# A row ring of fifteen slots instead of ten, and a weight ring of two blocks instead of three, in a streaming encoder layer with product-key experts

## What is computed

```
xn = rmsnorm(x);  z = xn @ w_in                       # 1024 -> 5632 columns
branch A: band attention, 8 heads of 64, own chunk of 64 and 8 chunks before, learned bias
branch B: HGRN2 gated recurrence, 4 heads, 128 x 128 state, exact chunkwise form
x = x + (sigmoid(ga) * (o_a @ w_a) + sigmoid(gb) * (o_b @ w_b)) @ w_out
PEER: q = rmsnorm(x) @ w_query; per head (8) two sets of 128 keys, top 16 of each,
      top 16 of the 256 sums -> 16 experts of 16384 per token and head, gates = softmax
      hid = gelu(x . u_tab[idx]);  out = sum over heads and experts of gate * hid * v_tab[idx]
y = rmsnorm(x + PEER)
```

## Time and profile before

| what | value |
|---|---|
| runs of the kernel (3) | 4533.14, 4541.51, 4547.78 us; median 4541.51 |
| profiled execution | 4581.09 us, span 4579.2 us |
| mean granted TensorE clock | 0.787 of full |
| busy, share of the span | TensorE 70%, VectorE 68%, GpSimd 58%, ScalarE 18% |
| DMA moved | 1408.39 MB, mean 308 GB/s |
| costliest groups | v rows on TensorE 1551.9 us; u rows on VectorE 1397.7 us; row fetches issued on GpSimd 1338.1 (v) and 1300.6 us (u); products on TensorE, L573, 775.8 us |

### The profile page before, as it was taken

How to read it: one execution, slowest core, us unless ns; L and a number is a source line. 1 busy time by engine, 2 the same in 40 slices (tenths; PEclk the granted TensorE clock), 3 DMA queues, 4 the chain that set the end, 5 groups by cost and what they waited for, 6 DMA issues and landing times. The chain is left out here.

```text
span 4579.2 us, 36423 instructions
## 1 busy us (share of the span) xinstructions
PE 3201.9 (70%) x11064; PEld 1997.1 (44%) x11064; DVE 3105.0 (68%) x6491; ACT 837.2 (18%) x2078; POOL 2656.9 (58%) x2349
## 2 busy tenths in 40 slices
PE   4968558896787567976874578858765677675555
PEld 3847314463464235643651256636432345343211
DVE  0142995647749976578579856685699765858865
ACT  1221112212111123121111222211111122111100
POOL 0001565646746676667456756575577765856776
PEclk7769657598888678987986698979876788787677
DMA  5415657989999899999998999989999999999998
GB/s 126 134 49 180 171 152 187 242 256 339 339 325 371 307 348 343 380 333 322 345 352 318 335 328 375 347 315 348 333 368 348 367 384 369 359 384 359 355 379 329
DMA packets 531664, 1408.39 MB, mean 308 GB/s; under 512 B 47952, under 2 KB 223568, under 8 KB 530704
## 3 DMA queue, kind: packets, MB, share of 16 engines
q0 software_dynamic: 317856, 1149.91, 70.2%
q1 hardware_dynamic: 211088, 246.98, 16.7%
q10 hardware_dynamic: 2528, 9.18, 0.5%
HBM read 1385.98 MB, written 19.92 MB: 307 GB/s over the span
## 5 line engine op out<-in xcount | busy, mean ns | idle before, releaser
L857 PE MATMUL PS<-ring,diag 128*128 128x512 f32 (+1 forms) x2304 | 1551.9, 814 | 963.8 <-DMA ring<-in_peer_v,idx 736.1
L557 POOL DMA_INDIRECT ring<-in_peer_v,idx x1152 | 1338.1, 1162 | 762.1 <-PE PS L857 394.1
L557 POOL DMA_INDIRECT ring<-in_peer_u,idx x1152 | 1300.6, 1129 | 721.9 <-DVE hid L1557 343.0
L1557 DVE CUSTOM_DVE_ANT_0 ring<-ring,xt 128x1024 f32<-128x1024 f32 (+1 forms) x1152 | 1397.7, 1221 | 416.3 <-DMA ring<-in_peer_u,idx 271.4
L857 PEld LDWEIGHTS PS<-ring,diag 128*128 128x128 f32 (+1 forms) x2304 | 503.0, 238 | 1733.5 <-issue 1548.6
L573 PE MATMUL PS<-xnT,wring 128*128 128x256 f32 (+2 forms) x3840 | 775.8, 364 | 131.4 <-DMA wring<-in_w_in 60.2
L1567 DVE SCALAR_TENSOR_TENSOR acc<-ring,wk,acc 128x1024 f32<-128x1024 f32 (+1 forms) x576 | 739.4, 1284 | 119.5 <-DMA ring<-in_peer_v,idx 86.1
L573 PEld LDWEIGHTS PS<-xnT,wring 128*128 128x128 f32 x3840 | 692.7, 202 | 251.3 <-issue 154.2
L543 POOL DMA_DIRECT2D xt<-xn_scr x9 | 5.5, 607 | 419.1 <-DMA xn_scr<-arena 419.0
L1173 ACT ACTIVATE diag<-ident,wk 128x128 f32<-128x128 f32 (+1 forms) x576 | 189.2, 384 | 73.4 <-issue 28.7
L577 PE MATMUL PS<-wring,xnT 128*128 128x256 f32 (+1 forms) x864 | 194.6, 384 | 8.0 <-DMA wring<-in_w_in 7.9
(11 more groups left out here) (179 smaller groups left out, 2620.3 us busy)
## 6 DMA issues: line engine op xcount, KB each, us to landing
wring<-in_w_in SPq DMA_DIRECT2D x110, 1024.0 KB
wring<-in_peer_query SPq DMA_DIRECT2D x40, 1024.0 KB
wring<-in_w_out SPq DMA_DIRECT2D x20, 1024.0 KB
ring<-in_peer_u,idx POOLq DMA_INDIRECT x1152
ring<-in_peer_v,idx POOLq DMA_INDIRECT x1152
bias<-rel_scr SPq DMA_DIRECT2D x80, 144.0 KB
wring<-in_w_branch_a SPq DMA_DIRECT2D x10, 1024.0 KB
wring<-in_w_branch_b SPq DMA_DIRECT2D x10, 1024.0 KB
```

Of the source, the lines that this page charges most:

```text
L557: pool.indirect_dma_start(ring[0:tile_rows[tn], n % R, :], None, u_tab if kind == "u" else v_tab, bass.IndirectOffsetOnAxis(ap=idx[0:tile_ ...
L857: mm = pe.matmul(PS[0:rows, 6 + half, :], diag[0:rows, seq % ND, 0:rows], ring[0:rows, n % R, 512 * half:512 * (half + 1)], start=(h == 0 ...
L1557: dve.tensor_tensor_reduce(row, row, xt[0:rows, s, :], 1.0, 0.0, ALU.mult, ALU.add, hid[0:rows, m % 2, k:k + 1]).then_inc(dve_used, 1)
```

## The change

- `R` 10 to 15 and `NW` 3 to 2. One weight block (8 KB a partition) and what the next two points free make room for five slots (20 KB a partition).
- `ND` 8 to 4: ScalarE makes diagonal j at k = max(0, 2j - 2) instead of max(0, 2j - 6).
- `idx` and `gates` keep four tiles' lists in place of nine (`LISTS`); the sample's keys and values lie in place 1 of `kT` and `v`.
- A slice holds one product instead of two, on all engines, with the cost table in the same proportion; VectorE's gating in D and G follows one product behind, not two. Stage F's first slice (the subtractions of all levels) becomes three, and the masking and the reduction of a head come into separate slices.

```diff
@@ -43,9 +43,10 @@
 CACHE = 2
-NW = 3
-R = 10
-ND = 8
+NW = 2
+R = 15
+ND = 4
+LISTS = 4
 ON_PE = frozenset(range(1, TOPK, 2))
@@ -65,13 +66,13 @@
     a = [6.0, 2.5, 0.5, 1.5, 0.5, 3.0] + [2.0] * nt
-    b = [3.5] * (4 + nt) + [2.0]
+    b = [1.7] * (8 + 2 * nt) + [2.0]
     c = [1.8] * (2 * (HA * nt + 3))
-    d = [1.5] + [2.5] * 8 + [0.5]
-    e = [3.5] * (4 + 2 * nt) + [0.5]
-    f = ([8.0, 4.5, 2.0] + [2.3, 1.5, 3.2] * HB + [1.0, 0.5, 2.0, 1.5]) * nt
-    gg = [2.5] * 8 + [0.5]
-    h = [3.5] * (2 * nt) + [0.5, 2.5, 0.5, 1.5, 3.0] + [1.5] * nt
+    d = [1.5] + [1.3] * 16 + [0.5]
+    e = [1.7] * (8 + 4 * nt) + [0.5]
+    f = ([2.5, 2.5, 3.0, 4.5, 2.0] + [2.3, 1.5, 1.2, 2.0] * HB + [1.0, 0.5, 2.0, 1.5]) * nt
+    gg = [1.3] * 16 + [0.5]
+    h = [1.7] * (4 * nt) + [0.5, 2.5, 0.5, 1.5, 3.0] + [1.5] * nt
     before = a + b + c + d + e + f + gg + h + [4.0]
@@ -257,8 +258,8 @@
         v = sb("v", [P, KV, DA])
-        kS = sb("kS", [P, CB, DEC])
-        vS = sb("vS", [P, DA])
+        kS = kT[:, :, P:P + DEC]
+        vS = v[:, 1, :]
         T12 = sb("T12", [P, 2, 2, DA])
@@ -270,8 +271,8 @@
 
-        idx = sb("idx", [P, NT * P], U32)
-        gates = sb("gates", [P, NT * P])
+        idx = sb("idx", [P, LISTS * P], U32)
+        gates = sb("gates", [P, LISTS * P])
         arena = sb("arena", [P, 5120 + 7680])
@@ -553,7 +554,7 @@
                     pool.wait_ge(dve_used if who == "dve" else pe_used, seq + 1)
-                at = tn * P + h * TOPK + k
+                at = tn % LISTS * P + h * TOPK + k
                 pool.indirect_dma_start(
@@ -613,8 +614,7 @@
                     product(n, xnT)
-                    if i % 2:
-                        yield
+                    yield
                 for n in by_stage[g, "B"][-2:]:
...
@@ -1040,16 +1035,17 @@
                     i.then_inc(pj_free[n % 2], 1)
-                    if i_ == 7:
+                    if i_ == 6:
                         act.wait_ge(f_fg, g + 1)
                         act.activation(Q[:, :, 0:W], K2[:, :, 0:W], ACT.Ln).then_inc(f_ln, 1)
-                    if i_ % 2:
-                        yield
+                    yield
                 leave()
...
                     ft = tile_no[g, ti]
+                    yield
+                    yield
                     yield
...
@@ -1176,7 +1173,7 @@
                     for j in range(len(ON_PE)):
-                        if k == max(0, TOPK // len(ON_PE) * j - 6):
+                        if k == max(0, TOPK // len(ON_PE) * (j - ND // 2 + 1)):
                             make_diag(m - 2, j)
@@ -1250,18 +1247,11 @@
 
-                for i, n in enumerate(by_stage[g, stage]):
-                    if products[n][4] == "branch":
-                        late.append(n)
-                    if i % 2:
-                        for q in late[:-2]:
-                            gate(q)
-                        now = late[-2:] if products[n][4] == "branch" else []
-                        if not now:
-                            for q in late:
-                                gate(q)
-                        late = now
-                        yield
+                for n in by_stage[g, stage]:
+                    for q in late:
+                        gate(q)
+                    late = [n] if products[n][4] == "branch" else []
+                    yield
                 for q in late:
...
@@ -1341,21 +1331,20 @@
                 for i_, n in enumerate(en):
-                    if i_ in (3, 5):
-                        for h in (i_ - 3, i_ - 2):
-                            n = en[h]
-                            dve.wait_ge(pj_free[n % 2], n // 2 + 1)
-                            i = dve.tensor_scalar(K2[:, h, 0:W], Q[:, h, 0:W], one_lb[:, h:h + 1], lb[:, h:h + 1],
-                                                  ALU.mult, ALU.add)
-                        if i_ == 5:
+                    if 1 <= i_ <= HB:
+                        h = i_ - 1
+                        n = en[h]
+                        dve.wait_ge(pj_free[n % 2], n // 2 + 1)
+                        i = dve.tensor_scalar(K2[:, h, 0:W], Q[:, h, 0:W], one_lb[:, h:h + 1], lb[:, h:h + 1],
+                                              ALU.mult, ALU.add)
+                        if i_ == HB:
                             i.then_inc(f_fg, 1)
-                    if i_ == 9:
+                    if i_ == 8:
                         dve.wait_ge(f_ln, g + 1)
...
                             dve.tensor_tensor_scan(Q[:, h, 0:W], restart[:, 0:W], Q[:, h, 0:W], 0.0, ALU.mult, ALU.add)
-                    if i_ % 2:
-                        yield
+                    yield
                 for n in en[-2:]:
@@ -1378,6 +1367,8 @@
                         dve.tensor_tensor(e4[:, :, :, 0, :], ref, c4[:, :, :, 0, :], ALU.subtract)
+                        if lev in (1, 3):
+                            yield
                     c3 = cum.rearrange("p h (b s) -> p h b s", s=CH)
@@ -1404,7 +1395,9 @@
                         at = PS[:, b0:b0 + 2, :].rearrange("p a (b t) -> p (a b) t", t=P)[0:rows, 0:NL + 1, 0:rows]
-                        link(dve.tensor_tensor(Am[0:rows, :, 0:rows], at, masks[0:rows, :, 0:rows], ALU.mult))
+                        i = dve.tensor_tensor(Am[0:rows, :, 0:rows], at, masks[0:rows, :, 0:rows], ALU.mult)
+                        yield
+                        link(i)
                         if fh >= 2:
@@ -1453,12 +1446,10 @@
                 hn = by_stage[g, "H"]
-                for i_ in range(0, len(hn), 2):
+                for i_ in range(len(hn)):
                     if i_:
-                        add_out(hn[i_ - 2])
                         add_out(hn[i_ - 1])
                     yield
-                add_out(hn[-2])
                 add_out(hn[-1])
...
```

More of the change, by code:

```diff
@@ L723, in mix @@
                     nch = rows // CH
-                    yield
-                    yield
+                    for _ in range(4):
+                        yield
                     if ti == 0:
@@ L1105, in mix @@
                 enter(act, g, "H")
-                for _ in range(2 * nt + 1):
+                for _ in range(4 * nt + 1):
                     yield
@@ L1287, in mix @@
                 enter(dve, g, "B")
-                for _ in range(4 + nt):
+                for _ in range(8 + 2 * nt):
                     yield
@@ L1526, in mix @@
                         link(dve.tensor_reduce(i12[r], eq[r], AX, ALU.add))
-                        at = tile_no[g, ti] * P + h * TOPK
+                        at = tile_no[g, ti] % LISTS * P + h * TOPK
                         dve.scalar_tensor_tensor(out=idx[r, at:at + TOPK], in0=i12[r, 0, :], scalar=128.0, in1=i12[r, 1, :],
@@ L1541, in unit @@
                     rows = tile_rows[m // PH]
+                    at = m % (LISTS * PH) * TOPK
                     dve.wait_ge(e_gelu, m + 1)
@@ L1545, in unit @@
                     dve.tensor_tensor(wk[0:rows, m % 2, :], glu[0:rows, m % 2, :],
-                                      gates[0:rows, m * TOPK:(m + 1) * TOPK], ALU.mult).then_inc(e_w, 1)
+                                      gates[0:rows, at:at + TOPK], ALU.mult).then_inc(e_w, 1)
                 elif kind == "R":
```

7 lines of the change are left out of this document (removed).

## The result

Over 8 runs each the changed kernel took 4574.47 us (4556.10 to 4579.62), the kernel before 4538.42 us (4533.14 to 4547.78): ratio 1.0066, interval 1.0047 to 1.0085. It is slower, by some 30 us by this ratio (the two medians lie 36 us apart). The forecast was 4519 us and faster.

A forecast was written before the change was run, and what follows sets the result against it. The DMA engines were taken as fullest overall, with the limit moving from engine to engine by stage. Terms of -84 - 10 + 66 + 5 = -23 us gave 4519 us from a median of 4541.51, range 4435 to 4625 for 8 in 10.

The forecast's parts named there:

- the weight ring's term: Weight loads in B, D, E, G and H: two blocks make weights late, 66 us lost, plus 5 us in group 0.
- ring of rows 10 to 15: Stages C, F and the start of I: five more rows fetched ahead, 20.9 us a group, 84 us gained.
- Single products and the small edits: All engines: finer slices -10 us; fewer scaling matrices, folded index lists and moved keys and values 0.
- tight block: Weight block whose load has little room: 22 a group (4 in B, 12 in D and E, 6 in G and H).
- the sum (-23): Whole kernel: -84 - 10 + 66 + 5 = -23 us on the profiled execution.
- Rival C: TensorE before a block's first product in B, D, E, G: late weights win at 2 us a block, 4629 us; chance 0.28.
- The window of 10.3 us: Stages D and E: with two blocks a load is wanted 10.3 us after issue; loads take 8 to 9 us.
- pauses in the stream: Weight loads under row fetches: 8 to 9 us a block holds only with pauses; the case without has 0.05.
- the waits of GpSimd would halve: GpSimd, 1026 to 4244 us: its waits for TensorE and VectorE fall to less than half of 586 us.
- Rival B: Row ring gains much more, half of the 250 us bound, weights cost a third (22 us): 4434 us; chance 0.25.
- Rival D: ScalarE: scaling matrices come late with four places, TensorE waits, its clock falls: +40 us, 4559 us; chance 0.12.
- Finer slices: All engines, one product a slice instead of two: between -40 and +20 us, taken as -10, near nothing.

The follow-up runs named there:

- e4: The kernel before with two weight blocks instead of three and nothing else changed; ratio 1.0184 to the kernel before, +83 us.
- e3: The changed kernel with three weight blocks instead of two and ten row slots instead of fifteen; ratio 0.9944 to the kernel before, -25 us.
- e1: The changed kernel with ten row slots instead of fifteen, all else of the change kept; ratio 1.0223 to the kernel before, +101 us.
- e2: The changed kernel with three weight blocks instead of two and thirteen row slots instead of fifteen; ratio 0.9836 to the kernel before, -74 us.
- e11: The changed kernel with weights in seven half blocks instead of two whole ones and twelve row slots instead of fifteen; ratio 0.9775 to the kernel before.

## Why the prediction was wrong

The step that failed is the weight ring's term: "I take 0.75 us a block, near the 1.07 and below it because a late weight stops TensorE, hence the gathers, and hands the DMA engines to the load", 66 us and with group 0 71, added to the other terms as if it did not depend on them. It does:

| term | forecast | measured with pairs | measured with single products |
|---|---|---|---|
| weight ring 3 to 2 | +71 | +83 (e4) | +126 (e3 to e1) |
| ring of rows 10 to 15 | -84 | not run | -71 (e1 to the change) |

Single products and the small edits were forecast at -10 us; they measured -25 with three blocks (e3) and +18 with two (e4 to e1). Either way round the parts add to +30 us, which is no test of them, since each is the difference of two neighbours in a chain of kernels from before to the change. Alone, in the kernel before, the price of the weight ring was nearly right: 83 / 88 = 0.94 us a tight block. In the changed kernel it is 126 / 88 = 1.4. The 43 us between the two are the largest miss (that number is known to some 16 us), and the sum had no term for it. Of the 53 us by which the sum (-23) missed +30, the ring of rows has 13; the rest is the weight ring and the single products together. Rival C, at 0.28, had the turning point at 1.0 us a block and is what happened, at seven tenths of its 2 us a block; its 4629 us were not reached, since the smaller price left +30 us of its +87.

What in that step does not stand up to the traces:

*The landing.* I took 8 to 9 us from two and three loads that stood one behind the other. That is a rate of a busy queue, not the time of one load. The page of e1 had a median of 10.7 us, that of the changed kernel has 12.1. All loads into the weight ring in stages D and E of the pass above:

```profile
DMA to landing us min/median/max: 4.9/10.4/17.5
```

The window of 10.3 us was right: about half of these loads landed within it and half not. With pairs (e4) the median of the page was 9.0 us, inside it, and 83 us were lost all the same; with three blocks (e3) it was 14.7 us, in a window of two periods. So the median alone does not tell the cost. The longest of this stretch stood alone in its queue, in stage E. Its issue, and what TensorE and GpSimd did meanwhile:

```profile
1952.42 0.37 SPq L436 DMA_DIRECT2D wring<-in_w_in  x1
```

```profile
1953.95 7.07 PE L574 MATMUL PS<-xnT,wring 128*128 128x256 f32 x32
1960.86 1.88 PE L854 MATMUL PS<-ring,diag 128*128 128x512 f32 x4
1970.01 10.16 PE L574 MATMUL PS<-xnT,wring 128*128 128x256 f32 x32 [7.27 <-DMA wring<-in_w_in]
```

```profile
1959.84 0.94 POOL L558 DMA_INDIRECT ring<-in_peer_v,idx  x1 [0.90 <-DVE hid L1549]
1963.01 0.94 POOL L558 DMA_INDIRECT ring<-in_peer_u,idx  x1 [2.23 <-PE PS L854]
1964.25 1.96 POOL L558 DMA_INDIRECT ring<-in_peer_v,idx  x1 [0.30 <-issue]
1966.51 0.93 POOL L558 DMA_INDIRECT ring<-in_peer_u,idx  x1 [0.30 <-issue]
1967.75 0.94 POOL L558 DMA_INDIRECT ring<-in_peer_v,idx  x1 [0.30 <-issue]
1982.16 0.93 POOL L558 DMA_INDIRECT ring<-in_peer_u,idx  x1 [13.47 <-PE PS L854]
```

It was issued at 1952.42 and its product started at 1970.01, 17.6 us later. GpSimd had issued five fetches from 1952.14 to 1958.94 with pauses of 0.30 us, and went on up to 1968.69 with none longer than 2.23 us. It had been wanted at 1970.01 - 7.27 = 1962.74, 10.3 us after its issue, just the window I had. The product before it had started without a wait, at 1953.95, so that block's load had landed by then and stood ahead of this one no longer. The rule of the Trainium skill that I had weighed (page "DMA: Bandwidth & Descriptors", section "Queues, rings and completion order") gave an estimate of 14 us beside an unbroken stream of rows; this load took longer still, and the median above, 10.4 us, is shorter. I had put 0.05 on it since I thought pauses in the stream the rule.

*The feedback.* I had counted that a late weight stops the gathers and so frees the DMA engines for the load. It does stop them, but late: TensorE stood still from 1962.74 on, GpSimd issued four more fetches up to 1968.69, and only then waited (13.47 us, the last row). By then the load had all but landed. And over the whole stretch GpSimd's waits became fewer with fifteen slots. Its waits for TensorE and VectorE from 1026 to 4244 us with ten slots (e1), to be set against 307.2 us in 86 waits and 263.8 in 78 above:

```profile
POOL ring L558 <- PE PS L854: 371.9, 110, 18.9
POOL ring L558 <- DVE hid L1549: 295.4, 92, 14.8
```

TensorE's waits for weights rose from 220.5 to 265.3 us between the two, and D and E took 28 us more over groups 1 to 4. With three blocks they rose as well, from 85.9 us with ten slots (e3) to 126.2 with thirteen (e2). So the deeper ring of rows makes weights later, which I had at nothing. That it did so by slower loads is not shown: over 1026 to 4244 us the median landing of all weight loads is 12.4 us in e1 and 12.2 in the changed kernel.

*The clock.* The granted clock before the wait of 7.27 us and after it:

```profile
1954.00:1961.00 7.00, 7.00 (x34) 6.17 (x33) 3.16 (x6) 0.67 (x2) 4.96 (x5) 1.00 1.03 386
1970.00:1980.00 10.00, 9.99 (x32) 8.30 (x33) 0.00 (x0) 0.38 (x1) 0.00 (x0) 0.70 0.51 194
```

It was 1.00 while TensorE was busy all the time, and 0.70 as a mean over the block behind the wait, which took 10.16 us in place of 7.07: 3.1 us more, not in my sum. Over D and E the mean fell from 1.00 to 0.94. I had the clock only in rival D. How much of the 126 us is the clock was not measured by itself; the waits alone grew by 135.

Point by point for the rest. The ring of rows: the sum was right in size (14 to 16 us a slot, 84 predicted for five and 71 measured), not in place, so the size is in part luck. By the marks, over groups 1 to 4 and from e1 to the change, B shrank by 39 us, F by 23, I by 16 and the tail by 11, while C grew by 13 and D and E by 28. I had given F 33 us, the start of I 18, C 32, and B nothing. (The two profiled executions lie 50 us apart, not 71, so these parts add to less.) That the waits of GpSimd would halve was wrong: the five slots took them from 667 us (e1) to 571, and they had been 586 before. Rival B (short waits go too, weights cost a third) is refuted by the +83 and +126 us of the weight ring. Rival D had TensorE's wait for scaling matrices double; it came near that, 171.9 to 308.0 us, but with six places instead of four the time stayed at 0.9836. That was tested with three blocks and thirteen slots; with two blocks and fifteen it was not, nor were eight places against four. The 358 GB/s of the Trainium skill's page "DMA: Bandwidth & Descriptors", section Specifications, were passed again: 359 GB/s over 3218 us in the row of e11 above, as a mean. Finer slices gained 25 us with three blocks and lost 18 with two, both inside the ends given (-40 to +20), though I had them as one number, -10.

Not settled: why single products make two weight blocks dearer (83 against 126 us). What the runs show is longer landings, longer waits and D as the main place; pairs in D and G alone did not bring the time back. And 0.9775 against 0.9791 does not tell seven halves from six.

## What to carry to other kernels

A buffer of a stream that shares the DMA engines with a fuller one needs to be sized by the longer landings of single loads under that traffic, not by the queue's rate: here a window of 10 us, with landings from 4.9 to 17.5 us in one pass of D and E, went with a loss of 83 to 126 us. When two rings compete for the same memory, cut the blocks of the one with few, large slots before taking one away: halves instead of whole blocks were worth 73 us for no memory. A stall on a full engine can cost more than its length: behind a wait of 7.27 us came a block that took 3.1 us longer at a lower granted clock. And two edits that are priced one by one need a run of the two together: here they were 43 us dearer than their sum.

## What was unexpected of the hardware

A lone load of 1 MB took 17.6 us from issue to the start of its product beside the row fetches, the longest of its stretch (the shortest landed in 4.9 us), and some 5 us or less without them. Twice as many DMAs of half the size did not cost more than they gained: six halves with thirteen slots took 0.9791, three whole blocks with thirteen slots 0.9836.
